# Eight half-token norms of a two-block transformer kernel, each cut into two steps of five and three tiles

## The reference

```
x = x + 0.5 * mx[2] * swiglu_2(modulate(rms_norm(x), mx[0], mx[1]), *ffn1)
...
h = modulate(rms_norm(x), mx[3], mx[4])
```

## Time and profile before

| | |
|---|---|
| median of 3 runs | 2589.32 us (2585.39 to 2589.62) |
| the profiled execution | 2593.13 us |
| its span, first to last instruction | 2591.3 us |
| TensorE busy | 2494.1 us (96%) |
| VectorE busy | 1335.6 us (52%) |
| ScalarE busy | 1035.0 us (40%) |
| mean granted TensorE clock | 0.985 of full speed |

### The profile page before, as it was taken

One profiled execution on the slowest core, in us unless ns is written; L12 is line 12 of the kernel. 1 busy time (PEld: TensorE's weight loads), 2 busy tenths in 40 slices (PEclk: granted clock), 3 DMA queues, 4 the chain that ended last, 5 costly groups with the idle time before them and its releaser, 6 DMA issues. The chain is left out here.

```text
span 2591.3 us, 37219 instructions
## 1 busy us (share of the span) xinstructions
PE 2494.1 (96%) x15710; PEld 2161.8 (83%) x15710; DVE 1335.6 (52%) x2198; ACT 1035.0 (40%) x1660; POOL 0.2 (0%) x4
## 2 busy tenths in 40 slices
PE   7999999989999999999888999999999998988999
PEld 6998789978998888888567888888888887878999
DVE  6657454655554333456886433335333337846553
ACT  5534444444433223146562322213222226744443
POOL 0000000000000000000000000000000000000000
PEclk9999999999999999999998999999999999999999
DMA  8986733488862333335102333333333336502564
GB/s 307 306 266 215 244 122 99 139 311 303 313 227 87 94 96 97 98 114 187 58 1 66 90 98 98 98 98 90 98 98 97 95 93 171 186 18 66 175 183 147
DMA packets 146727, 372.28 MB, mean 144 GB/s; under 512 B 20330, under 2 KB 67074, under 8 KB 146562
## 3 DMA queue, kind: packets, MB, share of 16 engines
q1 hardware_dynamic: 146274, 369.59, 44.4%
q10 hardware_dynamic: 288, 0.31, 0.1%
HBM read 368.71 MB, written 1.15 MB: 143 GB/s over the span
## 5 line engine op out<-in xcount | busy, mean ns | idle before, releaser
L298 DVE TENSOR_TENSOR weights_lo<-weights_raw,weights_hi 128x1024 fp32r<-128x1024 f32 (+2 forms) x547 | 657.4, 1212 | 485.0 <-ACT weights_hi L292 482.9
L350 PE MATMUL psum<-normed_hi,weights_hi 128*128 128x256 f32 (+2 forms) x2664 | 884.1, 332 | 22.6 <-DVE normed_lo L629 6.5
L350 PE MATMUL psum<-normed_lo,weights_hi 128*128 128x256 f32 (+2 forms) x2664 | 869.9, 327 | 0.0
L350 PE MATMUL psum<-normed_hi,weights_lo 128*128 128x256 f32 (+2 forms) x2664 | 869.3, 326 | 0.0
L292 ACT CAST weights_hi<-weights_raw 128x1024 fp32r<-128x1024 f32 (+2 forms) x547 | 562.7, 1035 | 374.1 <-DMA weights_raw<-in_w_down 254.3
L350 PEld LDWEIGHTS psum<-normed_hi,weights_hi 128*128 128x128 f32 (+1 forms) x2664 | 512.0, 192 | 86.0 <-issue 35.1
L350 PEld LDWEIGHTS psum<-normed_lo,weights_hi 128*128 128x128 f32 (+1 forms) x2664 | 513.2, 193 | 41.5 <-issue 1.2
L350 PEld LDWEIGHTS psum<-normed_hi,weights_lo 128*128 128x128 f32 (+1 forms) x2664 | 512.9, 193 | 40.7
L350 PE MATMUL psum<-hidden_hi,weights_hi 128*128 128x512 f32 (+1 forms) x594 | 217.6, 366 | 0.0
L350 PE MATMUL psum<-hidden_hi,weights_lo 128*128 128x512 f32 (+1 forms) x594 | 217.1, 365 | 0.0
L350 PE MATMUL psum<-hidden_lo,weights_hi 128*128 128x512 f32 (+1 forms) x594 | 217.0, 365 | 0.0
(11 more groups left out here) (264 smaller groups left out, 2724.1 us busy)
## 6 DMA issues: line engine op xcount, KB each, us to landing
weights_raw<-in_w_gu SPq DMA_DIRECT2D x220, 512.0 KB, 3.6
weights_raw<-in_w_down SPq DMA_DIRECT2D x110, 512.0 KB, 3.6
arena<-in_w_mod SPq DMA_DIRECT2D x72, 512.0 KB, 7.1
weights_raw<-in_w_x SPq DMA_DIRECT2D x24, 512.0 KB, 7.4
resid<-in_w_mod SPq DMA_DIRECT2D x24, 512.0 KB, 7.6
normed_raw<-in_w_mod SPq DMA_DIRECT2D x24, 512.0 KB, 6.9
under_normed_hi<-in_w_mod SPq DMA_DIRECT2D x24, 512.0 KB, 7.2
weights_raw<-in_w_qk SPq DMA_DIRECT2D x24, 512.0 KB, 3.7
```

The source lines that it names most:

```text
L298: ve.tensor_tensor(w_lo[:, c % RING, a], w_raw[:, c % RING, a], w_hi[:, c % RING, a].bitcast(F32), ALU.subtract).then_inc(lo_ready, 1)
L350: last = te.matmul(out, a, b, start=start and n == 0, stop=stop and n == 2)
```

## The change

`Norm` gets an argument `parts`. With `parts=2` it has two steps: the first does all that comes ahead of the tiles, scale 0 to 4, hi 0 to 4 and lo 0 to 3; the second does scale 5 to 7, hi 5 to 7 and lo 4 to 7. TensorE's part of a norm is issued in the first step alone. `in_halves` makes its norms with two parts, and `joined` puts one product step between the two steps of each norm: the last but one step of `down` in the first norm, the second of `up_steps` in the second. No instruction is added or taken away. Every other norm keeps one part.

```diff
-            def __init__(self, a, gain, shift, into=None, squares_at=None, summed=None, first_chunk=False):
+            def __init__(self, a, gain, shift, into=None, squares_at=None, summed=None, first_chunk=False, parts=1):
+                self.n = parts
...
+            def tiles_of(self, i):
+
+                if self.n == 1:
+                    return range(KD + 1)
+                return range(KD // 2 + 1) if i == 0 else range(KD // 2 + 1, KD + 1)
+
             def tensor(self, pe, i):
+                if i:
+                    return
...
             def scalar(self, act, step, i):
+                if i == 0:
+                    self.root(act, step)
+                if self.in_place:
+                    return
+                for k in self.tiles_of(i):
+                    if k == KD:
+                        continue
+                    act.wait_ge(norm_vv, self.vv0 + 2 + k)
...
+            def vector(self, dve, step, i):
+                if i == 0:
+                    self.mean(dve, step)
                 dest = resid if self.in_place else normed_raw
-                for k in range(KD + 1):
+                for k in self.tiles_of(i):
...
-            return [modulated(layer, shift, shift + 1, half, summed=n)
+            return [modulated(layer, shift, shift + 1, half, summed=n, parts=2)
...
-            steps = steps_of(down)
-            return [*steps[:1 - HALVED], (norms[0], 0), *steps[1 - HALVED:], up_steps[0], (norms[1], 0), *up_steps[1:]]
+            steps, at = steps_of(down), 1 - HALVED
+            return [*steps[:at], (norms[0], 0), steps[at], (norms[0], 1), *steps[at + 1:],
+                    up_steps[0], (norms[1], 0), up_steps[1], (norms[1], 1), *up_steps[2:]]
```

More of the change, by code:

```diff
@@ L568, in scalar, with root @@
             def scalar(self, act, step, i):
+                if i == 0:
[6 more added lines that the diff above has]
+                    act.wait_ge(norm_vv, self.vv0 + 2 + k)
+                    if self.shift is None:
+                        last = se.copy(normed[0][:, k, self.a], normed_raw[:, k, self.a])
+                    else:
+                        for side in self.sides:
+                            a = slice(side * S, (side + 1) * S)
+                            last = se.activation(normed[0][:, k, a], normed_raw[:, k, a], ACT.Identity,
+                                                 bias=self.shift(k, side))
+                    last.then_inc(norm_av, 1)
+            def root(self, act, step):
                 if self.squares_at is not None:
@@ L580, in scalar, with mean @@
                 se.activation(r, r, ACT.Exp, scale=-0.5).then_inc(norm_av, 1)
[L581 to L594, removed]
+            def mean(self, dve, step):
                 w = self.a.stop - self.a.start
@@ L632, in vector, with modulated @@
                         last.then_inc(normed_ready, 1)
-        def modulated(layer, shift, scale, a, squares_at=None, summed=None):
+        def modulated(layer, shift, scale, a, squares_at=None, summed=None, parts=1):
             return Norm(a, lambda k, s: mod[:, (layer * NMOD + scale) * KD + k, s:s + 1],
                         lambda k, s: mod[:, (layer * NMOD + shift) * KD + k, s:s + 1], squares_at=squares_at,
-                        summed=summed)
+                        summed=summed, parts=parts)
         class FfnUp(LinearF):
```

## The result

The changed kernel takes 2595.55 us (median of 18 runs, 2589.22 to 2600.24), the kernel before beside it 2590.61 (18 runs): +4.94 us, ratio 1.0021, interval [1.0013, 1.0028]. It is slower, as forecast (2595.2 us), by 0.2%. The profiled execution took 2595.13 us, its span was 2593.4. In the code of after, the lines named ahead of the prediction are: L560 now L570 (norm sum), L606 now L624, L616 now L638 (scale), L590 now L592 (hi), L629 now L651 (lo); L292, L298, L350, L481, L526 stay.

A forecast was written before the change was run, and what follows sets the result against it. TensorE, busy 96% of the span, was taken as the bound. Joints A, B and C, 1.2 + 2.33 + 2.33 = +5.9 us, led from 2589.32 to 2595.2 us (+0.23%), 8-in-10 range 2587.5 to 2598.8.

The forecast's parts named there:

- TensorE's waits bound what can be won or lost: Whole kernel: TensorE is busy 96% of the span, so reordering VectorE and ScalarE can win no more than its waits.
- First norms 0: First norms of all joints: cutting them costs 0; in B a 1.4 us delay is hidden by the wait for squares.
- Second norm of D 0: Joint D: the step between is a `grid_load`, SP's alone, so 0; its wait of 2.1 us stays.
- 2.33 us of lateness for one split: Second norms of A, B, C: scale 5 starts 2.33 us later, 1.19 VectorE standing for a cast, 1.14 the split.
- Joint C +2.33: Joint C, second norm: TensorE takes late tiles as they come, so their whole lateness costs +2.33 us.
- longer pauses bring stretches of their own: Rival, joints A and C: longer pauses bring half-clock stretches, one adds 1.7 us, two 3.4; 2596.9 to 2598.6 us; 14%.
- counted the clock on neither side: All joints: a gap of some 2.2 us costs 1.7 us at half clock in some executions, nothing in others; left out.
- Joint B, +0.45 to +2.33, taken at +2.33: Joint B, second norm: +0.45 us against the profiled execution with its half-clock stretch, +2.33 at full clock; the upper end taken.
- the rival that I gave 8%: Rival: A's pause and stretch go, B's stretch goes with its pause broken in two, no tile late; -5.8 us, 2583.5; 8%.
- Joint A +1.2: Joint A, second norm: weights wait goes, 3.4 us wait for L481's bank comes; +1.2 us, from -0.5 to +2.9.
- The sum, +5.9: Whole kernel: terms of joints A, B and C, 1.2 + 2.33 + 2.33, added to the median of 2589.32 us.
- the 0.2% that the prediction held to be the least that can be told: Whole kernel: measurement can tell about 0.2%, 5.2 us, from no change; the forecast lay just beyond it.

The follow-up runs named there:

- e1: Only the first norm of each joint cut into five and three tiles, second whole; ratio 0.9996 against the kernel before.
- e9: Four second norms with the product step between tiles 4 and 5 on ScalarE alone, VectorE in its old order; ratio 0.9998 against the kernel before.
- e2: Only the second norm of each joint cut, first whole; ratio 1.0018 against the kernel before.
- e3: Only the second norms of joints B and C cut, which lead into the feed-forward products; ratio 1.0018 against the kernel before.
- e5: As e3, but two product steps between the parts instead of one; ratio 1.0040 against the kernel before.
- e6: Only the second norms of A and D cut, and in c_k's steps ScalarE reads finished sums ahead of its weight cast; ratio 0.9999 against the kernel before.
- e7: Second norms of A and D moved, first part behind the fourth product step, second behind the fifth, other norms whole; 2590.86 us against 2591.42 before.
- e10: As e7, but cut behind tile 2 and the second part behind the sixth product step; 2587.88 us against 2590.47 before.
- e8: As e7, with the first norm of B cut too; 2591.16 us, ratio 1.0000 against the kernel before.
- e11: As e10, with B's first norm cut too, into three and five tiles; 2586.92 us against 2590.47 before.
- e12: As e11, but the second part behind the eighth product step in A and the seventh in D; 2582.06 us against 2588.00 before.

## Why the prediction was right, point by point

- *TensorE's waits bound what can be won or lost.* Held. Of the six waits for squares, though, two belong to other norms (at 531 and 2389 us), not one; nothing rested on it.
- *First norms 0.* The medians agree (e1). In B's traces (after, e1) it was less than nothing: of the pause of 2.23 us for squares 0.79 was left, a pause of 1.43 for lo 4 came ahead of it, and the half-clock stretch of the earlier trace rows was gone.
- *Second norm of D 0.* Held: 37.31 us in both.
- *2.33 us of lateness for one split, 1.19 of it standing and 1.14 the split.* Held: 1.12 of standing, 1.15 from the split's start to scale 5, lo 7 +2.34; TensorE's wait ahead of tile 4 was 1.52 (forecast near 1.7). That it is VectorE's standing and split, and not the cast, e9 shows.
- *Joint C +2.33.* The mechanism held, the size didn't: the joint grew by 3.84. The term left out is a half-clock stretch of the joint's own, behind the late tiles. Windows of PE in after, joint C, from tile 4 on:

```profile
1796.32:1799.06 2.74, 2.34 (x13) 1.00 0.02 6
1799.06:1802.48 3.42, 3.42 (x19) 0.50 0.49 153
```

  3.84 less 2.34 is 1.50 for it (1.50 in e2, too; 1.13 in e3 and 0.51 in e5, where more of it falls on time in which TensorE would have waited for the tiles). The four traces in which C's second norm is cut on both engines (after, e2, e3, e5) all have it, the ten others none. So the rival "longer pauses bring stretches of their own" was right in this joint, where I had counted the clock on neither side.
- *Joint B, +0.45 to +2.33, taken at +2.33.* Both ends were about right: with the stretch on both sides 41.98 to 42.55 (e2), +0.57; without one on either 39.87 (e1) to 42.22 (after), +2.35. The choice was not. It rested on the profiled execution being 3.81 us above its median, which says nothing of where the stretches lie: eight of nine traces whose first norm of B is whole have a stretch at half clock there, none of the five with the cut. From before to after the joint went from 41.98 to 42.22, +0.24: the second norm's loss was nearly paid by the stretch that the first norm's cut took away, part of the rival that I gave 8%.
- *Joint A +1.2, 3.4 us of wait for L481's bank in place of the one for weights.* Held: 3.24 us, +1.16 at full clock (e2 against e3), and e6 shows ScalarE's queue as its place. After's trace has 6.83 us at a granted 0.50 there (1153.94 to 1160.77) where before's has 3.41 (1155.57 to 1158.98), so its A grew by 2.24.
- *The sum, +5.9.* Measured +4.94 [3.4, 7.3]. It came out through two misses that cancel in part, by the lengths of the traces: C's term was 1.5 too small, B's 2.1 too large. And 2589.32 was a low start: in 18 runs the kernel before took 2590.61. The mechanism of the lateness is shown; that the total fell 0.35 us from the forecast is luck. The interval is also narrower than the 0.2% that the prediction held to be the least that can be told: it spans 0.15% in all.
- *The Trainium skill, TensorE: Matmul & The Clock Gate (Why this matters for your kernels).* By its rule a long enough pause between bursts of matmuls brings the lower clock. The traces agree only in part: with A's pause of 3.2 us two of three have a stretch (not e2), with its pause of 2.0 to 2.3 us four of six (not e3 and e6), with D's 2.1 three of nine; and C's late tiles have it in three of three with pauses of 1.52, 0.17 and 0.17, and in e5 with one of 2.64.

## What to carry to other kernels

In a list that all engines go through in order, a step put inside another one costs more than its instructions last on the engine that is held up: here 1.12 of the 2.3 us were VectorE waiting for a cast that ScalarE had only just begun, and with VectorE's order left whole the same cast cost 0.43 (e9). Cutting a long step pays where its second part is not needed soon, and then only if the reads that free TensorE's banks, and the splits due next, stand ahead of it; otherwise the wait comes back under another name, as in e7. So after every move ask what stands first behind the moved part on each queue, and check the sum of the waits up to the end of the following products rather than the one wait that went.

## What the hardware showed beyond that

In 14 traces of nearly the same work TensorE's time at half clock lay between 61.4 us (12 stretches, e6) and 85.3 us (18, e5; 17 in e10), and joint A, which all of them reach by the same code, began between 1119.96 and 1125.32 us. Traces of nearly the same work thus differ by as much as the effect measured here.

How a pause is broken up went with the clock as much as its length did. One pause of 2.23 us ahead of the sum of squares of B's second norm was followed by a granted 0.50 in eight of nine traces. Broken up, with matmuls between, it was so in none of five: in three of these (after, e1, e8) the pauses were 1.43, 0.17, 0.17 and 0.79, in two (e11, e12) 0.57, four times 0.17, and 0.79. No median shows the worth of that.
